# A bidirectional encoder block: the output projection by Strassen's scheme over pairs of token tiles

## The reference

```python
h = rmsnorm(x, norm1_g)
z = h @ w_in
za, zb = z[..., :512], z[..., 512:]          # 4 heads of 128, 4 groups of 128
ya = fourier_mix(za, w_fourier)              # FFT over tokens and channels, real part, @ w_fourier
yb = pool_mix(zb, w_pool, pool_scale)        # centred means of 2, 4, 8, 16 tokens, minus zb, @ w_pool
x = x + concat([ya, yb], -1) @ w_out
h = rmsnorm(x, norm2_g)
x = x + (silu(h @ w_gate) * (h @ w_up)) @ w_down      # d_ff = 2816
return rmsnorm(x, normf_g)
```

## Time and profile before

| | |
|---|---|
| median of 3 runs (lowest, highest) | 2560.36 us (2560.03, 2561.17) |
| profiled execution: time | 2562.66 us |
| its span (first to last instruction) | 2560.9 us |
| granted TensorE clock, mean | 0.999 |
| PE, DVE, ACT busy | 99%, 61%, 35% of the span |
| `project_out` on PE | about 382.8 to 665.2 us |
| the FFN's first tile on PE | 665.2 to 688.1 us |

### The profile page before, as it was taken

One profiled execution on the slowest core, in us unless ns is written; L12 is line 12 of the kernel. 1 busy time (PEld: TensorE's weight loads), 2 busy tenths in 40 slices (PEclk: granted clock), 3 DMA queues, 4 the chain that ended last, 5 costly groups with the idle time before them and its releaser, 6 DMA issues.

```text
span 2560.9 us, 32494 instructions
## 1 busy us (share of the span) xinstructions
PE 2541.0 (99%) x11600; PEld 2112.4 (82%) x11600; DVE 1564.8 (61%) x2482; ACT 883.6 (35%) x1583; POOL 141.9 (6%) x200
## 2 busy tenths in 40 slices
PE   8999999999999999999999999999999999999998
PEld 6888888888788888888888888888888888888887
DVE  4322584444877677687677687767764664554665
ACT  5333344333633333333333343333332332233333
POOL 1434600000000000000000000000000000000000
PEclk9999999999999999999999999999999999999999
DMA  4313444556732232432232252222236664453554
GB/s 190 113 76 115 146 172 169 212 201 234 275 122 106 80 123 106 168 132 106 80 120 106 93 206 107 94 106 106 97 137 243 242 226 135 153 181 132 195 200 152
DMA packets 129599, 381.54 MB, mean 149 GB/s; under 512 B 9968, under 2 KB 15344, under 8 KB 120304
## 3 DMA queue, kind: packets, MB, share of 16 engines
q1 hardware_dynamic: 121536, 350.61, 38.0%
q0 software_dynamic: 7984, 29.89, 3.0%
HBM read 253.85 MB, written 126.62 MB: 149 GB/s over the span
## 4 chain that ended last, share of the span: by engine, by line
PE 99%; ACT 0%; DVE 0%; issue 0%; DMA 0%; ACTq 0%
PE bank L307 32%; PE bank L309 32%; PE bank L308 32%; PE bank L1043 1%; PE bank L1417 1%; PE bank L544 1%; PE bank L1104 0%; ACT junk L418 0%; DMA xin<-in_x 0%; PE bank L599 0%; DVE uv_lo L956 0%; ACT uv_hi L881 0%; ACT xin L470 0%; ACT win_hi L467 0%; DVE h_lo L505 0%
## 5 line engine op out<-in xcount | busy, mean ns | idle before, releaser
L307 PE MATMUL bank<-a_hi,w_hi 128*128 128x512 f32 x1848 | 719.2, 389 | 2.4 <-issue 2.4
L309 PE MATMUL bank<-a_hi,w_lo 128*128 128x512 f32 x1848 | 719.0, 389 | 0.0
L308 PE MATMUL bank<-a_lo,w_hi 128*128 128x512 f32 x1848 | 718.9, 389 | 0.0
L307 PEld LDWEIGHTS bank<-a_hi,w_hi 128*128 128x128 f32 x1848 | 346.8, 188 | 75.3 <-issue 3.2
L309 PEld LDWEIGHTS bank<-a_hi,w_lo 128*128 128x128 f32 x1848 | 346.8, 188 | 72.0
L308 PEld LDWEIGHTS bank<-a_lo,w_hi 128*128 128x128 f32 x1848 | 346.9, 188 | 71.9
L307 PE MATMUL bank<-t_hi,s_hi 128*128 128x512 f32 x924 | 359.4, 389 | 0.0
L308 PE MATMUL bank<-t_lo,s_hi 128*128 128x512 f32 x924 | 359.4, 389 | 0.0
L309 PE MATMUL bank<-t_hi,s_lo 128*128 128x512 f32 x924 | 359.4, 389 | 0.0
L1756 ACT ACTIVATE w_hi<-t_raw 128x512 fp32r<-128x512 f32 x256 | 161.9, 632 | 465.2 <-PE bank L309 395.9
L2145 DVE TENSOR_TENSOR s_lo<-s_raw,s_hi 128x512 fp32r<-128x512 f32 x231 | 156.1, 687 | 231.8 <-ACT s_hi L1855 231.8
(11 more groups left out here) (172 smaller groups left out, 2936.2 us busy)
## 6 DMA issues: line engine op xcount, KB each, us to landing
s_scr<-sums_out SPq DMA_DIRECT2D x33, 1792.0 KB, 5.9
s_raw<-s_scr SPq DMA_DIRECT2D x42, 1024.0 KB, 5.1
w_raw<-in_w_gate SPq DMA_DIRECT2D x64, 512.0 KB, 3.6
w_raw<-in_w_up SPq DMA_DIRECT2D x64, 512.0 KB, 4.4
wd_staged<-in_w_down SPq DMA_DIRECT2D x121, 256.0 KB
a_raw<-ha_scr SPq DMA_DIRECT2D x21, 1024.0 KB, 4.8
s_raw<-s_scr SPq DMA_DIRECT2D x21, 768.0 KB, 4.7
x<-in_x SPq DMA_DIRECT2D x24, 512.0 KB, 6.4
```

The lines of the kernel that those rows point to most:

```text
L307: pe.matmul(out, w_hi, m_hi, start=first, stop=False, **checks)
L308: pe.matmul(out, w_hi, m_lo, start=False, stop=False, **checks)
L309: return pe.matmul(out, w_lo, m_hi, start=False, stop=last, **checks)
```

## The change

Tiles 0 to 3 stay as they are. From tile 4 on, two tiles make a pair, pairs n = 2 to 11 (`LAST`). The pair's y is a 2x2 matrix of blocks (rows: the two tiles; columns: halves of the 1024 channels), `w_out` another (512x512 blocks). Seven block products of 12 matmuls replace eight. For that DVE makes four differences T1 to T4 of `w_out` blocks once, in place over the raw rows (128x2048 each); ACT rounds them and DVE takes their remainders, T1 and T2 beside tiles 1 to 3, T3 and T4 in pair 2. For each pair DVE makes S1 to S4 of y blocks; ACT rounds and DVE splits seven 128x512 operands; ACT copies the first product out to `U`; DVE adds U, `u4` and x, and then a bank to each quarter of `x1` (`c11`, `c22`, `c12`, `c21`). The scaling of `xn` moves from DVE to ACT (`scaled`), `h_out` has two slots instead of four and `h_sums` one in the loop, y is loaded by pairs (1.05 MB), x1 is stored as soon as its sums are in, and at the end SP issues the FFN's first operands as products of the last pair end, and the last x1 stores behind them. In `first_tile` the transposes of tile 22 stand before product 3, those of tile 23 behind it. The orders, cut to what carries them (the start on DVE, loads and stores of y, x and h, and renamed semaphores are left out):

```diff
+    T1, T2, T3, T4 = range(4)
+    T_PARTS = ((0, 0), (1, 1), (0, 1), (1, 0))
+    t_raw = [w_raw[i][:, c, :, :] for i, c in T_PARTS]
...
+
+        at = par * PAIR + tile * P
+        return y_raw[:, 4 * rows:4 * rows + 4, at:at + P]
...
+            sp.wait_ge(x1_ready, m * 2 + (3 - slot % 2 if not (isinstance(m, int) and m < 4) else 2))
+            sp.dma_start(x1_scr[bass.ds(m * P, P), :], x1[:, slot, :]).then_inc(x1_stored[slot], DMA)
+
+        def next_x(m, slot, rounds):
+
+            sp.wait_ge(xn_ready, m + 1)
+            sp.wait_ge(x1_stored[slot], rounds * DMA)
+            load_x(m + 4, slot)
...
+        def pair(n):
+            k, par = n // 2, n % 2
+            before, slot = k - 1 + par, 2 * (1 - par)
+            store_x1(2 * n - 2, slot)
+            if n + 2 <= LAST:
+                sp.wait_ge(y_ready, split(n, A22))
+                load_y(n + 2, par)
+            next_x(2 * n - 2, slot, before + 1)
+            store_x1(2 * n - 1, slot + 1)
+            next_x(2 * n - 1, slot + 1, before + 1)
+            store_h(n - 1, 1 - par)
...
+        store_x1(NT - 4, 0)
+        for par in range(2):
+            sp.wait_ge(h_stored[par], 2 * 3 * DMA)
+        store_x1(NT - 3, 1)
+        sp.wait_ge(pair_ready, product_of(LAST, 1))
         load_a(0)
+        feed.first_weights(0)
+        sp.wait_ge(pair_ready, product_of(LAST, 2))
         load_a(1)
-        store_x1(last, 0)
-        sp.wait_ge(o_ready_half, 2 * (NT - 3))
-        for e in range(2):
-            for part, w in enumerate((w_gate, w_up)):
-                sp.dma_start(ahead.raw[:, e, part * D:(part + 1) * D], w[e * (FT // 2)]).then_inc(ahead.raw_loaded[e], DMA)
-        store_h(2 * last - 1, 1)
-        sp.wait_ge(o_ready_half, 2 * (NT - 2))
+        sp.wait_ge(pair_ready, product_of(LAST, 3))
         load_a(2)
-        store_x1(last, 1)
-        store_x1(last, 2)
-        sp.wait_ge(o_ready_half, 2 * NT - 1)
+        load_a(4)
+        sp.wait_ge(pair_ready, product_of(LAST, 4))
         load_a(3)
-        load_a(4)
-        sp.wait_ge(o_ready_half, 2 * NT)
+        store_h(LAST - 1, 0)
         load_a(5)
+        sp.wait_ge(pair_ready, product_of(LAST, 5))
         load_a(6)
-        store_h(2 * last, 0)
-        store_x1(last, 3)
+        store_x1(NT - 2, 2)
+        feed.first_weights(1)
+        store_x1(NT - 1, 3)
         feed.second_weights()
-        store_h(2 * last + 1, 1)
+        store_h(LAST, 1)
...
+        def round_t(t):
+            act.wait_ge(t_summed, (T1, T3, T2, T4).index(t) + 1)
+            if t in (T3, T4):
+                act.wait_ge(tile_ready, 4)
+            act.activation(t_hi[t][:, :, :], t_raw[t], ACT.Copy).then_inc(t_hi_done, 1)
...
+        def round_v(n, k, par, v):
...
+        def root(m, slot):
+            act.wait_ge(var_ready, m + 1)
+            act.activation(std[:, slot:slot + 1], var[:, slot:slot + 1], ACT.Sqrt).then_inc(std_ready, 1)
+
+        def scaled(m, slot):
+            act.wait_ge(rstd_chain, m * 4 + 4)
+            act.activation(xn[:, slot % 2, :], x1[:, slot, :], ACT.Copy, scale=rstd[:, slot:slot + 1]).then_inc(xn_ready, 1)
...
+        def copy_product(n):
+            act.wait_ge(pair_ready, product_of(n, 0))
+            act.activation(U[:, :], o_ps[0][:, :], ACT.Copy).then_inc(p_copied, 1)
...
+        round_y(2)
+        round_t(T1)
+        squares(0, 0, 2)
+        root(0, 0)
+        scaled(0, 0)
+        round_y(3)
...
+        def norms_before(n, par):
+            slot = 2 * (1 - par)
+            first = isinstance(n, int) and n == 2
+            squares(n * 2 - 2, slot, n * 4 - (2 if first else 1))
+            root(n * 2 - 2, slot)
+            scaled(n * 2 - 2, slot)
+            squares(n * 2 - 1, slot + 1, n * 4)
+            root(n * 2 - 1, slot + 1)
+
+        def pair(n, k, par):
+            slot = 2 * (1 - par)
+            round_v(n, k, par, A22)
+            norms_before(n, par)
+            copy_product(n)
+            if isinstance(n, int) and n == 2:
+                round_t(T3)
+                round_t(T4)
+            after, k_after = n + 1, k + par
+            round_v(after, k_after, 1 - par, A11)
+            scaled(n * 2 - 1, slot + 1)
+            stage_h(n * 2 - 2, slot, (h_stored[par], k * (3 * DMA)))
+            round_v(after, k_after, 1 - par, S1)
+            stage_h(n * 2 - 1, slot + 1)
+            for v in (S2, A12, S3, S4):
+                round_v(after, k_after, 1 - par, v)
+
+        in_turn(act, pair)
+        round_v(LAST, NT // 4 - 1, 1, A22)
+        norms_before(LAST, 1)
+        copy_product(LAST)
+        scaled(NT - 3, 1)
+        stage_h(NT - 4, 0, (h_stored[1], (NT // 4 - 1) * (3 * DMA)))
+        stage_h(NT - 3, 1)
+        act.wait_ge(y_ready, split(LAST, A22))
+        feed.round_a(0, 0)
+        act.wait_ge(pair_ready, product_of(LAST, 4))
+        feed.round_w(0, 0, 0, 0)
+        feed.round_w(0, 0, 0, 1)
+        feed.round_a(0, 1)
+        feed.round_w(0, 0, 0, 2)
+        squares(NT - 2, 2, 2 * NT - 1)
+        feed.round_a(0, 2)
+        root(NT - 2, 2)
+        squares(NT - 1, 3, 2 * NT)
+        feed.round_w(0, 0, 0, 3)
+        feed.round_a(0, 3)
+        scaled(NT - 2, 2)
+        act.wait_ge(xn_ready, NT - 1)
+        feed.copy_first()
+        root(NT - 1, 3)
+        scaled(NT - 1, 3)
+        feed.round_a(0, 4)
+        stage_h(NT - 2, 2, (h_stored[0], (NT // 4) * (3 * DMA)))
+        feed.round_w(0, 0, 0, 4)
+        feed.round_a(0, 5)
+        stage_h(NT - 1, 3)
+        feed.round_w(0, 0, 0, 5)
+        feed.round_w(0, 0, 0, 6)
+        feed.round_a(0, 6)
+        feed.round_w(0, 0, 1, 0)
+        feed.silu_first()
+        feed.second_tile()
...
+        def sum_t(t):
+
+            a, b, op = {T1: (w_raw[0][:, 1, :, :], t_raw[T1], ALU.subtract), T3: (w_raw[1][:, 1, :, :], t_raw[T3], ALU.subtract),
+                        T2: (t_raw[T2], t_raw[T1], ALU.subtract), T4: (t_raw[T4], t_raw[T2], ALU.subtract)}[t]
+            order = (T1, T3, T2, T4)
+            if t != T1:
+                dve.wait_ge(t_summed, order.index(t))
+            dve.tensor_tensor(t_raw[t], a, b, op).then_inc(t_summed, 1)
+
+        def rest_of_t(t):
...
+            a11, a12, a21, a22 = part(par, 0, 0), part(par, 1, 0), part(par, 0, 1), part(par, 1, 1)
+            a, b, op = {S1: (a21, a22, ALU.add), S2: (v_raw[S1][:, :, :], a11, ALU.subtract), S3: (a11, a21, ALU.subtract),
+                        S4: (a12, v_raw[S2][:, :, :], ALU.subtract)}[v]
+            dve.tensor_tensor(v_raw[v][:, :, :], a, b, op).then_inc(v_summed, 1)
...
+        def rest_of_v(n, par, v):
+            dve.wait_ge(y_hi_done, rounded(n, v))
+            src = {A11: part(par, 0, 0), A12: part(par, 1, 0), A22: part(par, 1, 1)}.get(v, v_raw[v][:, :, :])
+            dve.tensor_tensor(v_lo[v][:, :, :], src, v_hi[v][:, :, :].bitcast(F32), ALU.subtract).then_inc(y_ready, 1)
...
+        def u_sums(n, k, par):
+
+            dve.wait_ge(pair_ready, product_of(n, 2))
+            dve.wait_ge(p_copied, n - 1)
+            dve.tensor_tensor(U[:, :], o_ps[1][:, :], U[:, :], ALU.add).then_inc(u_summed, 1)
+            dve.wait_ge(u_summed, u_of(n, 0))
+            dve.tensor_tensor(u4[:, :], o_ps[2][:, :], U[:, :], ALU.add).then_inc(u_summed, 1)
+            for tile in range(2):
+                dve.wait_ge(x_loaded[2 * par + tile], k * DMA + DMA)
+            for i, (tile, c) in enumerate(((0, 1), (1, 0))):
+                at = quarter(par, tile, c)
+                dve.tensor_tensor(at, at, U[:, :], ALU.add).then_inc(u_summed, 1)
+            dve.wait_ge(u_summed, u_of(n, 1))
+            at = quarter(par, 1, 1)
+            dve.tensor_tensor(at, at, u4[:, :], ALU.add).then_inc(u_summed, 1)
+
+        def add_bank(n, par, j, bank, tile, c):
+
+            dve.wait_ge(pair_ready, product_of(n, j))
+            if (tile, c) != (0, 0):
+                dve.wait_ge(u_summed, u_of(n, {(0, 1): 2, (1, 0): 3, (1, 1): 4}[tile, c]))
+            at = quarter(par, tile, c)
+            dve.tensor_tensor(at, o_ps[bank][:, :], at, ALU.add).then_inc(x1_ready, 1)
+
+        def c11(n, par):
+            add_bank(n, par, 3, 0, 0, 0)
+
+        def c22(n, par):
...
+        def norms_before(n, par):
+            slot = 2 * (1 - par)
+            if isinstance(n, int) and n == 2:
+                residual(3)
+            else:
+                c21(n - 1, 1 - par)
+            variance(n * 2 - 2, slot)
+            rest_of_v(n, par, A22)
+            inverse(n * 2 - 2, slot)
+            variance(n * 2 - 1, slot + 1)
+
+        def pair(n, k, par):
+            slot = 2 * (1 - par)
+            after, k_after = n + 1, k + par
+            norms_before(n, par)
+            rest_of_v(after, 1 - par, A11)
+            inverse(n * 2 - 1, slot + 1)
+            if isinstance(n, int) and n == 2:
+                rest_of_t(T3)
+            sum_v(after, k_after, 1 - par, S1)
+            u_sums(n, k, par)
+            if isinstance(n, int) and n == 2:
+                rest_of_t(T4)
```

(126 more changed lines are left out.)

436 lines of the change are left out of this document (207 added, 229 removed).

## The result

The changed kernel takes 2566.36 us (median of 20 runs, 2563.72 to 2569.67), the kernel before beside it 2560.95 (20 runs): 5.4 us more, ratio 1.0020, 95% interval 1.0013 to 1.0027. The forecast was 2561.4 with a range of 2545 to 2569. So the time is inside the range, 2.6 us from its upper end, and 5.0 us above the forecast. It lies above 2565.5, in the part that the prediction called slower and gave 0.27, at the lower end of rival 4's times. The profiled execution of after took 2568.57 with a span of 2566.8.

What follows compares the result with a forecast made beforehand. PE, busy 99% of the span, was taken as the bound. Matmuls -27.3, loop +8.8, pair 2 +7.4 and seam +12.2 sum to +1.1 us on 2560.36: forecast 2561.4 us, range 2545 to 2569.

Steps and rivals of the forecast that it cites:

- the part that the prediction called slower: Whole kernel: outcomes above 2565.5 us, chance 0.27, from slow seam transfers or upper costs of pair 2 and clock.
- rival 4: Seam to the FFN: transfers at 325 GB/s or less delay tile 22's x1 store; 2566 to 2570 us, chance 0.18.
- The matmuls: PE in the ten pairs: 120 matmuls fewer at 0.2273 us each, 27.3 us less.
- The loop: Second transposes wait for the odd tile's norm: 0.94 us in pairs 4 to 10, 2.2 in pair 3; 8.8 more.
- both fit in 20.9, so neither is the bound by its sum: Per pair: DVE's 16.8 us and ACT's 13 us of work fit within PE's 20.9; only order can hurt.
- Rival 2: Pairs' loop runs without waits, handovers or scaling being shorter than taken: 8 us less, 2553 us, chance 0.10.
- Pair 2: Rounding T3 and T4 costs 4.5 us before second transposes, their remainders 2.9 before A22: 7.4 us more, bounds 5 and 9.
- The seam: FFN's first tile waits for tile 22's queued x1 store: 14.7 us of waits, 12.2 more than before.
- L: Landing of tile 22's x1 store, put 15 us after the FFN began; product 3 starts 3.9 us later.
- the clock: Lower PE clock after the wait before product 3: taken as 0, with 0.8 us kept for the range.
- (1): Tile 22's x1 store passes the loads instead of queueing: seam costs 6 us less, 2555 us, chance 0.14.
- (3): No loop waits and no queued store together, or nearly the full gain: 2533 to 2546 us, chance 0.10.

Runs made afterwards that it cites:

- e6: The kernel before with 120 matmuls left out and nothing added, x1 incomplete: 2544.58 us, ratio 0.9937 to before.
- e3: The changed kernel, pairs 3 to 10 with the second tile's norm put first on ACT and DVE: 2570.73 us, ratio 1.0043 to before.
- e4: The changed kernel, pairs 3 to 10 with ACT's and DVE's work reordered over the whole pair: 2558.91 us, ratio 0.9993 to before.
- e1: The changed kernel with the last two x1 stores issued earlier on SP's queue, ahead of h store, loads and weights: 2557.07 us, ratio 0.9985 to before.
- e9: The changed kernel with x1 stores ahead, pairs 2 to 10 reordered, and seam a_hi and a_lo made as early as possible: 2545.72 us, ratio 0.9938 to before.

## Why the prediction was right, and where its steps were not

**The matmuls.** 120 fewer at 0.2273 us: right as PE's work, 27.3. But e6 shows that 27.3 us less of PE's work shorten the stage and the seam by 19.6 even in the order of before (16.1 in the whole kernel, see above). The prediction treated the removal and the waits as two terms; part of the waits belongs to any shorter tile. Its sum was not hurt, since it priced the waits of the new order directly.

**The loop.** 8.8 predicted, 8.2 measured. Predicted was 0.94 late in a pair; measured were 0.64 to 0.74 of idle in pairs 4 to 9 and 0.51 in pair 10, plus a slow first matmul behind each, 0.94 in all between the two rows shown. The chain named was the right one. What the text said beside it, that "both fit in 20.9, so neither is the bound by its sum", held too, and e3 against e4 shows the other half: moving the late link alone loses 4.4 us, moving it into a hole gains 7.5. Rival 2 falls.

**Pair 2.** 7.4 predicted (4.5 + 2.9), 7.2 measured (4.0 + 0.16 before the transposes, the rest ahead of A22). Of the second part, e1 shows 1.4 as a wait and the other 1.6 as matmuls at the lower clock; in after nearly all is such matmuls, and the wait of 3 us that the prediction wanted to see before A22 isn't there. The clock was not in the prediction here; it cost next to nothing, because A22 would have waited for DVE in any case. That the total came out is owed to the right moment for DVE's c22, not to the right picture of PE.

**The seam.** This is the step that was mis-sized: 14.7 in the first tile predicted, 19.6 measured, and 12.2 more than before predicted, 16.5 measured. Its mechanism is the one named: `copy_first` at the landing, product 3 at L + 3.9. Two sizes were off. One is the landing: L came 17.4 us behind the FFN's start (670.50 - 653.12), not 15. The first load went out 5.5 us after the last pair's start, as taken. The rate was as taken, too:

```profile
637.80:670.50 32.70, 25.07 (x120) 19.94 (x118) 20.03 (x33) 18.86 (x35) 0.00 (x0) 0.94 0.97 370
```

But 370 GB/s over 32.7 us are 12.1 MB, not the 10.75 that the prediction counted up to this store. The 1.57 MB issued behind it (two weight loads and the x1 store of tile 23) make 12.3. So nearly all of what stood behind the store had been moved by the time that it landed, and the first of these, issued at 654.5, landed a microsecond before it:

```profile
w_raw<-in_w_gate SPq DMA_DIRECT2D x1, 512.0 KB, 15.0
w_raw<-in_w_up SPq DMA_DIRECT2D x1, 512.0 KB, 17.6
```

A count of the bytes issued ahead was too small a term, by some 2.4 us. Why the queue didn't finish in its order isn't shown. The other is the clock, which I took as 0: product 3 took 5.3 us instead of 2.73, of which product 4's wait swallowed all but 0.3 (0.8 expected). But the late transposes held up ACT's staging and by it product 5 (2.58 of wait against 1.38 in e1), and product 5 itself ran at the lower clock again from 687.1 on, 4.4 us against 2.73; product 6 then had no wait (0.41 in e1). Some 2.7 us together. The Trainium skill, "TensorE: Matmul & The Clock Gate", section "HAM oscillation", has a PE that waits for transfers between bursts start the next one at the lower clock. The trace agrees: behind the 10.57 us of wait matmuls start 0.43 us apart, not 0.23. The slack that I set against it covered one product and not the work that other engines do behind the transposes.

**The rivals.** (1) was wrong as put: behind the loads the store landed after 16.3 us, ahead of them after 3.5, and 1.05 MB more ahead of it cost 2.5. (4) gave the right time, 2566 to 2570, but not by its mechanism: the rate wasn't lower than 370 GB/s, and the seam's transfers cost 2.4 us more because bytes behind the store went with it; the clock added the rest. The range held the time for a similar reason: it was wide enough for 344 GB/s, and for a clock that was to cost 0.8 and cost 2.7. That part is luck. (3), the near full gain, exists, but takes four reorderings: 2544.7, as much as the bare removal brings.

## What to carry to other kernels

When a change shortens the engine that bounds, price the removal together with the other engines' timetable at the new pace, and lay that out in order of the code: it gave pair 2 and the loop within 0.6 us each, and e4's time in its range. It has to hold the last operations of a stage too: it overlooked the 2.57 in e9. Of a late link, ask what the engine does while it waits elsewhere in the same period; filling such a hole is worth what moving the link alone is not. A small store that frees a buffer belongs ahead of the bulk loads that it does not need. Behind them it can wait even for bytes issued after it.
